# A hybrid GLA / convolution / PEER layer on one core: another order of the loads and stores on SyncE's queue

## The reference, cut to what matters

```python
qf = (xt @ w_q).reshape(T, 8, 2, 128)
s = jnp.einsum('thpd,hpnd->thpn', qf, sub_keys)
sv, si = lax.top_k(s, 16)
cand = sv[:, :, 0, :, None] + sv[:, :, 1, None, :]
top_s, pos = lax.top_k(cand.reshape(T, 8, 256), 16)
gate = softmax(top_s)
act = gelu(einsum('td,thkd->thk', xb, u_tab[ib]))
out = einsum('thk,thkd->td', gb * act, v_tab[ib])
```

## Time and profile before

| | us |
|---|---|
| median of 3 runs | 3996.21 |
| lowest, highest | 3987.92, 3999.82 |
| the profiled execution, its own time | 3999.82 |
| its span in the trace | 3997.8 |
| PE busy | 3436.8 (86%) |
| DVE busy | 2896.0 (72%) |
| mean DMA rate over the span | 317 GB/s |

### The profile page before, as it was taken

How to read it: one execution, slowest core, us unless ns; L and a number is a source line. 1 busy time by engine, 2 the same in 40 slices (tenths; PEclk the granted TensorE clock), 3 DMA queues, 4 the chain that set the end, 5 groups by cost and what they waited for, 6 DMA issues and landing times.

```text
span 3997.8 us, 32340 instructions
## 1 busy us (share of the span) xinstructions
PE 3436.8 (86%) x9517; PEld 1739.0 (43%) x9517; DVE 2896.0 (72%) x6406; ACT 993.0 (25%) x2518; POOL 1065.8 (27%) x950
## 2 busy tenths in 40 slices
PE   6877899986778888577777699999999999989998
PEld 3336344432353444224445344444445444445444
DVE  1535787846736796898898687787778877866666
ACT  1212321336241211117668111111111111111111
POOL 0000222312212232332230233333333333333332
PEclk9998899987889999788886799999999999999999
DMA  5334666766748789898892899999999999999997
GB/s 205 121 142 171 219 249 213 263 220 221 260 172 311 293 306 360 324 402 317 348 351 109 345 412 412 401 405 409 407 410 399 411 404 405 407 370 413 401 409 288
DMA packets 255863, 1268.04 MB, mean 317 GB/s; under 512 B 25620, under 2 KB 76052, under 8 KB 136646
## 3 DMA queue, kind: packets, MB, share of 16 engines
q0 software_dynamic: 131504, 958.53, 61.1%
q1 hardware_dynamic: 122744, 302.20, 20.1%
q10 hardware_dynamic: 1440, 5.24, 0.3%
HBM read 1216.30 MB, written 49.58 MB: 317 GB/s over the span
## 4 chain that ended last, share of the span: by engine, by line
PE 56%; DVE 19%; DMA 18%; issue 4%; ACT 3%; SPq 0%; DVEq 0%; POOL 0%; ACTq 0%
PE bank L1070 12%; PE wide L1082 9%; DMA arena<-in_uv 8%; PE bank L1029 6%; DMA ring_e<-in_uv,idx 5%; PE bank L834 5%; PE bank L1082 4%; PE wide L789 4%; PE bank L857 3%; PE bank L998 2%; DMA arena<-in_ut 2%; PE bank L981 2%; DVE ring_e L1666 2%; DVE arena L1726 2%; PE bank L802 2%
## 5 line engine op out<-in xcount | busy, mean ns | idle before, releaser
L1070 PE MATMUL bank<-arena 128*128 128x384 f32 x2048 | 688.2, 490 | 42.0 <-DMA arena<-in_ut 41.0
L735 POOL DMA_INDIRECT arena<-in_uv,idx x384 | 438.5, 1142 | 972.0 <-PE bank L1029 614.3
L1726 DVE CUSTOM_DVE_ANT_0 arena<-arena,h2e 128x1024 f32<-128x1024 f32 x384 | 462.1, 1221 | 211.6 <-DMA arena<-in_uv,idx 210.8
L711 POOL DMA_INDIRECT ring_e<-in_uv,idx x256 | 302.6, 1182 | 1039.1 <-PE wide L789 526.7
L1070 PEld LDWEIGHTS bank<-arena 128*128 128x128 f32 x2048 | 391.8, 192 | 344.8 <-issue 76.6
L1082 PE MATMUL wide<-arena 128*128 128x512 f32 x1024 | 481.8, 615 | 50.6 <-DMA arena<-in_uv 50.5
L735 POOL DMA_INDIRECT ring_e<-in_uv,idx x256 | 301.5, 1178 | 589.7 <-PE bank L1029 378.3
L1363 ACT ACTIVATE small<-small 128x4 f32<-128x4 f32 x160 | 32.9, 205 | 1660.5 <-DVE small L1726 1639.4
L1666 DVE CUSTOM_DVE_ANT_0 ring_e<-ring_e,h2e 128x1024 f32<-128x1024 f32 x256 | 308.4, 1222 | 175.6 <-DMA ring_e<-in_uv,idx 174.9
L1726 DVE CUSTOM_DVE_ANT_0 ring_e<-ring_e,h2e 128x1024 f32<-128x1024 f32 x256 | 307.8, 1220 | 140.6 <-DMA ring_e<-in_uv,idx 140.6
L1082 PEld LDWEIGHTS wide<-arena 128*128 128x128 f32 x1024 | 199.9, 197 | 314.3 <-issue 246.6
(11 more groups left out here) (259 smaller groups left out, 4660.7 us busy)
## 6 DMA issues: line engine op xcount, KB each, us to landing
arena<-in_ut SPq DMA_DIRECT2D x128, 512.0 KB
arena<-in_uv SPq DMA_DIRECT2D x128, 512.0 KB
arena<-in_w_q SPq DMA_DIRECT2D x48, 512.0 KB
spread_d<-arena SPq DMA_DIRECT2D x12, 2048.0 KB
arena<-spread_d SPq DMA_DIRECT2D x96, 256.0 KB
ring_e<-in_w_mod POOLq DMA_DIRECT2D x8, 2048.0 KB, 8.2
arena<-in_w_cols SPq DMA_DIRECT2D x24, 512.0 KB
arena<-in_x SPq DMA_DIRECT2D x20, 512.0 KB, 3.7
```

The costliest lines, as they stand in the source:

```text
L711: pool.indirect_dma_start(out=ring_e[k % ERING], out_offset=None, in_=a["uv"], in_offset=bass.IndirectOffsetOnAxis(ap=idx[k // SLOTS][:, k ...
L735: pool.indirect_dma_start(out=ring[r], out_offset=None, in_=a["uv"], in_offset=bass.IndirectOffsetOnAxis(ap=idx[kept(t)][:, k:k + 1], axis ...
L1070: ins = pe.matmul(s_bank[:, 0:NC], lhsT=utb[i % URING][:, k * P:(k + 1) * P], rhs=H2T[1][:, k, P:P + NC], start=(k == 0), stop=(k == KD - 1))
L1726: dve.tensor_tensor_reduce(out=ring[r][:, 0:D], in0=ring[r][:, 0:D], in1=h2b[kept(t)], scale=1.0, scalar=0.0, op0=ALU.mult, op1=ALU.add, a ...
```

## The change

Three places on SP's queue change, and no other engine's instructions do.

```diff
-                        if hp >= 4 and hp % 4 == 3:
+                        if hp >= 4 and hp % 4 == 1:
                             store_scores(sp, b, tb, n, hp // 4 - 1)
...
-                c = slice(part * SPANS, (part + 1) * SPANS)
+                c = slice(part * CN, (part + 1) * CN)
...
-            sp.wait_ge(*S["g_out0"].at(CN * SPANS - 2))
+            for g in range(CN * SPANS - 2, CN * SPANS):
+                sp.wait_ge(*S[f"g_out{g % 2}"].at(g))
             load_u(0)
-            sp.wait_ge(*S["g_out1"].at(CN * SPANS - 1))
-            for part in range(GPARTS):
+            for part in range(NG):
                 load_gates(0, part)
...
                 if i + 2 < ETILES:
                     load_u(i + 2)
-                if i // NG + 1 < ETILES // NG and i % NG < GPARTS:
-                    load_gates(i // NG + 1, i % NG)
                 if i + 1 < ETILES:
                     load_v(i + 1)
+                if i // NG + 1 < ETILES // NG:
+                    load_gates(i // NG + 1, i % NG)
```

More of the change, by code:

```diff
@@ L60 @@
 NG = 4
-GPARTS = CN
 SPAN = 32
```

## The result

The changed kernel takes 4046.68 us (median of 4 runs, 4042.76 to 4055.63), the kernel before, run beside it, 3997.88 us (4 runs). The ratio is 1.0138, with an interval of 1.0115 to 1.0160. The change costs 49 us where I had forecast 10, and the time lies above the upper end of my range, 4045.

A forecast was written before the change was run, and what follows sets the result against it. Bytes through the DMA engines were taken to set the last stage's pace. Block 0 4.2, blocks 1 and 2 0 + 4, start 1.5, stage 0: 9.7 us on the median 3996.2 gave 4006 us, range 3980 to 4045.

The forecast's parts named there:

- Block 0: Front: chunk loads behind the earlier score stores land late, three PE waits of 1.4 us, 4.2 us in sum.
- Blocks 1 and 2: Front: PE has slack against DVE; block 1 costs 0, block 2 three chunks 1.3 us late, 4 us.
- The start: Start of last stage: first `u` waits for both spans, delaying the second `u`; 1.5 us, bounds 0 and 7.1.
- The last stage: Gates in four parts behind `v`: some `v` waits become gates waits, bytes and best rate unchanged, so 0 us.
- The rival of the late gates: Last stage: gates' last part becomes the wait at `weigh`, PE after it; halfway 32 us, 4038 us; chance 0.22.
- The rival of the even parts: Last stage: even parts put less in front of the worst `v`; 27 us gained, 3979 us; chance 0.20.
- The hidden front: Front: chunk loads land in time, start covered, only 2 us of block 0 remain; 3998 us; chance 0.13.
- the three signs by which I would have called myself wrong: PE's waits for `weigh` above 90 us, stage shorter by over 20 us, or PE never waiting for `in_w_q` in block 0.

The follow-up runs named there:

- the wait without the store: Kernel before, where SP waits for DVE's fourth score at the new, earlier place but issues the store at the old one: 4006.27 us, ratio 1.0024.
- the first edit alone: Kernel before with only the score stores moved two weight loads earlier: 4028.27 us, ratio 1.0080.
- the new layout: Kernel before with `spread_d` laid out by groups of four expert tiles, gates read in 2 KB pieces, span stores written in 512 bytes: 3972.37 us, ratio 0.9940.

## Why the prediction was wrong, step by step

**Block 0: right.** I forecast three waits of 1.4 us and 4.2 us in sum. The trace has 4.4 us, and the run with this block alone has three waits of 3.9 us in sum and a time 4.8 us longer (0 to 10 by its interval).

**Blocks 1 and 2: the step that failed.** I had put them at 0 + 4 us; they cost 29.5. The mechanism was the forecast's, a chunk that stands behind a store and lands late. Its size was not, for two reasons.

First, the landing time. I took the middle between the landing "alone" and "gathers take every second turn". From the first store's issue to PE's product the six chunks took 11.8, 12.8 and 9.3 us in block 1 (upper end of my bound 11.9), and 13.8, 13.4 and 11.3 us in block 2 (upper end 13.4). The upper ends were the rule, not the worst case. Against the due times of the forecast, 9.95 us after the store in block 1 and 8.8 in block 2, these six are 1.8, 2.9, 0, 5.0, 4.6 and 2.5 us late, 16.8 us in sum. There was a reason to choose longer ones: the row of the gather that took 11.81 us in the chain right there said that the engines were contended at this time, and I used the durations of the earlier trace rows, of other loads, without asking how loaded the engines were. The chunks themselves, 512 KB as well, take 8.1 us in the median in the kernel with the start alone changed, where I had 3.7.

Second, I gave the slower product no price. After the five long waits the query product took 8.78, 9.03, 8.79, 9.58 and 9.29 us, and 7.13 after the short one, 52.6 in sum, against 6 x 7.03 = 42.2, so 10.4 us more. Together with the 16.8 this makes 27.2 of the 29.5 us.

PE's own balance over the two blocks, from `in_sk` to the scores read back, closes it: PE is busy 10.9 us longer (276.9 against 266.0) and idle 18.6 us longer. It waits 38.6 us more for chunks (39.2 against 0.6), but its waits for ACT ahead of the score products have shrunk from 23.7 to 1.1 us. So the slack that I counted on was there, and took up more than half of the waits. Waits short of it cost nothing visible, as the wait without the store shows; only what went beyond it was paid.

**The start.** 1.5 us forecast, no difference measured, and the interval (-5 to 8 us) can't tell the two apart.

**The last stage: wrong.** I took 0 from the argument that bytes and best rate stay the same. The edit costs 16 us. From the first gates to the end the stage lasts 1790 to 1792 us in all three traces with 512 byte pieces behind `v` and 1768 to 1782 in the seven with them ahead of it, at a mean DMA share of 0.99 in the former and 0.99 to 1.00 in the latter. So the engines moved the same bytes in a longer time and were no less busy: with a full share the rate was no constant of this stage, it moved with the order. PE's products wait 100 to 103 us in the former and 79 to 93 in the latter. I also had the number that speaks against the new place. The gates used to be issued 7.7 us ahead of the next load in the queue, and now the next `u` follows them 5.2 us behind, by the trace of before; after the change it is 4.8 us, from 3057.41 to 3062.20. I noted it and gave it no price.

**The rival of the late gates** was right in what happens and half right in size. DVE waits for 27 groups, 186.7 us in sum, and the parts in the two chains shown take 20.8 and 23.8 us to land, near the 24.93 that I had from the worst `v`. But PE's waits for `weigh` are 26.8 us (35.8 with the gates alone), not over 90, since most of a wait of 6.9 us is hidden in the slack between the end of `weigh` and `sum_rows`, 6.0 us in step 60 (3068.6 - 3062.07 - 0.55). Late `weigh` is not all that a waiting DVE costs: PE also waits 16.3 us in the changed kernel for DVE's L1695 at the ends of two gathered tiles, 4.6 us with the gates alone, and not at all before. On the other side the waits for `v` are gone. I put the halfway price at 32 us; all of the gates' edits cost 16, and how much of it is this rival's is not shown. My price also took the 89 us of the stage as what PE waits already, which fits its products' waits of 50.5 and 41.0 us; the 67.8 that I named beside the 41.0 are waits of the weight loads. I set "slower by the gates" beside a front that costs 10, and never both upper ends together; that is why the range missed.

**The rival of the even parts** is refuted by the run with four parts ahead of `v`: ratio 0.9994 (27 us less would be 0.993, the interval ends at 0.9978), waits for `v` 70.2 us. In the changed kernel the waits for `v` did go, and the time was lost elsewhere. **The hidden front** is refuted by the first edit alone.

**What would have shown me wrong.** PE waits three times for chunks in block 0, as said. The last stage starts 33 us later, not 10; that is where the trace contradicts the forecast first. The stage lasts 8.2 us longer than in the one trace of before, but 16.8 longer than the mean of six, more than the 10 that I allowed. DVE waits once in four steps, up to 12.4 us where I had said 10. None of the three signs by which I would have called myself wrong came true: PE's waits for `weigh` are under 90 us, the stage is not shorter, and PE waits in block 0. I had named none for blocks 1 and 2, where most was lost.

The Trainium skill ("DMA: Bandwidth & Descriptors", Specifications) gives 512 bytes as the least size of a transfer that reaches the full rate. Here the trace disagrees in part: reading the gates in 2 KB instead of 512 byte pieces shortened the landing from 18.8 to 10.6 us and the stage by 27 us. The same page (Why small descriptors are slow) says that each packet carries a fixed overhead besides its bytes, and the direction of this result agrees with that. No run here tells the fixed overhead from the time that many small pieces wait for the gathers between them. What the prediction took from this page needs two limits. The fit of 2.0 us plus bytes / 436e3 stands there for DMAs that GpSimd issues, and the stores and loads here are SP's. And the turns between queues go by packets, which by the page hold 9 to 17 descriptors as a rule, so that each small piece waits for a turn of its own was my inference.

## What to carry to other kernels

Ahead of the load with the least lead, keep the queue free of anything that waits or is large: here nine stores of 0.25 to 1 MB, each put in front of a 512 KB load, cost 32 us with their bytes and 10 us with the wait alone. Where a late load shares the engines with gathers, take the contended duration as the forecast and the lone one as the bound. Where the engines are full, look at the pieces and not only at the bytes: a layout that made the small pieces larger where the engines are full, and smaller in a store where they are not, was worth 24 us, more than any order of the queue tried here. Check forecasts of a full stage against more than one trace: the profiled execution of before had the longest stage of seven.

## What the runs showed of the hardware that I had not expected

- After PE had stood still for 6.4 to 7.8 us, the product behind it took 8.8 to 9.6 us at a mean granted clock of 0.74 to 0.81 instead of 7.03 at 1.00. In the wait without the store it took 9.87 us at 0.72 after 6.0 us, and 7.13 at 1.00 after 3.6 and after 2.0 us. The longer product adds 1.7 to 2.8 us to a long wait, but of both together the kernel pays only what goes beyond PE's slack.
- At a DMA share of 0.98 to 1.00 the mean rate over the whole stage was 395 GB/s with gates of 512 byte pieces behind `v`, 397 to 400 with them ahead of it, and 404 to 405 with the new layout.
- 512 byte pieces in a span store of 2 MB cost some 5 us each (15.9 against 10.5 us), twelve times. Of this the start of the stage shows only what the last store adds: the first gates go out 9.4 us behind the first `u` (2227.37 against 2218.01), where it was 7.1 before.

Open are the last 5 us of the wait without the store, how the 16 us of the gates' edits divide between the place behind `v` and the part in the group's last step, whether the new layout gains by the size of the pieces or by where they lie, and why the chunks of the third store in each block land somewhat sooner (9.3 and 11.3 us) than the others.
